# Softmax transposes of a decoder layer: from TensorE to 32x32 pieces on VectorE, blocks 2 to 7

## What is computed

```
h   = rms_norm(x, ln_mix_g) @ w_in
y_a = rms_norm(spatial_gating(h[..., :IN_A], ...), grp_norm_a)      # chunks of 128 tokens
y_b = rms_norm(short_gated_conv(h[..., IN_A:], conv_w), grp_norm_b) # width 3, causal
x   = x + concatenate([y_a, y_b], -1) @ w_out
# cross-attention, 4 heads, 256 memory tokens
q = rms_norm(x, ln_attn_g) @ w_q ; k, v = split(memn @ w_kv)
s = einsum("bshd,bmhd->bhsm", q, k) * scale
p = softmax(s, axis=-1)
x = x + einsum("bhsm,bmhd->bshd", p, v) @ w_o
# SwiGLU
g, u = split(rms_norm(x, ln_ffn_g) @ w_gate_up)
x = x + (silu(g) * u) @ w_down
return rms_norm(x, ln_final_g)
```

## Time and profile before

| what | before |
|---|---|
| median of 3 runs | 1652.73 us |
| profiled execution, own time | 1653.19 us |
| its span, slowest core (others from 1637.3) | 1651.7 us |
| TensorE busy | 1599.9 us, 97% |
| VectorE busy | 879.0 us, 53% |
| ScalarE busy | 725.9 us, 44% |
| mean granted TensorE clock, slowest core | 0.990 |
| matmuls of L1178 (transposes) | 256 |

### The profile page before, as it was taken

One profiled execution on the slowest core, in us unless ns is written; L12 is line 12 of the kernel. 1 busy time (PEld: TensorE's weight loads), 2 busy tenths in 40 slices (PEclk: granted clock), 3 DMA queues, 4 the chain that ended last, 5 costly groups with the idle time before them and its releaser, 6 DMA issues.

```text
span 1651.7 us, 22422 instructions; the slowest of 8 cores (1637.3 to 1651.7 us)
## 1 busy us (share of the span) xinstructions
PE 1599.9 (97%) x7916; PEld 758.7 (46%) x7916; DVE 879.0 (53%) x1414; ACT 725.9 (44%) x1291; POOL 76.0 (5%) x152
## 2 busy tenths in 40 slices
PE   5988999999899999999999999999999999999997
PEld 2454444444344444444444444444444444444456
DVE  4777783246455565636655565456645466433324
ACT  3644655114375246543464435554455434531221
POOL 2000000010000000000000000000000000000000
PEclk9999999999999999999999999999999999999999
DMA  9785847879997898889867994658747375334741
GB/s 213 115 167 131 205 96 130 147 129 202 214 226 124 163 222 236 169 165 176 240 183 189 168 236 176 209 119 176 234 178 232 97 183 197 128 112 155 254 168 52
DMA packets 44349, 285.64 MB, mean 173 GB/s; under 512 B 4944, under 2 KB 6992, under 8 KB 21200
## 3 DMA queue, kind: packets, MB, share of 16 engines
q0 software_dynamic: 20032, 122.95, 43.4%
q1 hardware_dynamic: 24208, 161.26, 27.5%
HBM read 365.20 MB, written 38.27 MB: 244 GB/s over the span
## 4 chain that ended last, share of the span: by engine, by line
PE 91%; DMA 7%; ACT 1%; DVE 1%; issue 1%; POOL 0%; DVEq 0%; SPq 0%; ACTq 0%; POOLq 0%
PE ps L614 64%; PE ps L1400 16%; PE ps L1127 7%; PE ps L1388 2%; DMA big<-x 2%; DMA big<-w_gate_up 2%; DMA big<-w_v 1%; DMA big<-w_qT 1%; PE ps L1178 1%; DMA big<-w_down 1%; PE ps L690 0%; DVE big L744 0%; PE ps L1069 0%; PE ps L1463 0%; DMA fold<-big 0%
## 5 line engine op out<-in xcount | busy, mean ns | idle before, releaser
L614 PE MATMUL ps<-big 128*128 128x512 bf16 (+1 forms) x5280 | 1158.0, 379 | 17.7 <-DVE big L820 5.4
L614 PEld LDWEIGHTS ps<-big 128*128 128x128 bf16 x5280 | 517.1, 98 | 626.6 <-issue 33.9
L662 ACT ACTIVATE big<-big 128x512 f32<-128x512 f32 (+1 forms) x320 | 192.0, 610 | 375.0 <-DVE big L940 256.5
L1400 PE MATMUL ps<-big 128*128 128x512 bf16 (+1 forms) x1424 | 278.8, 354 | 0.7 <-DMA big<-w_down 0.7
L1334 DVE TENSOR_TENSOR big<-ps,big 128x512 bf16<-128x512 f32 x176 | 120.4, 689 | 225.5 <-PE ps L614 176.8
L940 DVE TENSOR_TENSOR big<-ps,big 128x512 f32<-128x512 f32 x184 | 127.1, 691 | 167.9 <-PE ps L614 84.5
L672 DVE TENSOR_TENSOR big<-big 128x512 f32<-128x512 f32 (+2 forms) x272 | 178.8, 666 | 59.7 <-ACT big L662 56.5
L1400 PEld LDWEIGHTS ps<-big 128*128 128x128 bf16 x1424 | 138.9, 98 | 132.3 <-issue 1.6
L744 DVE SCALAR_TENSOR_TENSOR big<-big 128x512 bf16<-128x512 f32 (+3 forms) x256 | 172.0, 721 | 48.0 <-ACT big L702 31.8
L1328 ACT ACTIVATE big<-ps 128x512 f32<-128x512 f32 x176 | 102.8, 594 | 161.5 <-PE ps L614 158.7
L1127 PE MATMUL ps<-big 128*128 128x512 bf16 x512 | 115.2, 379 | 0.0
(11 more groups left out here) (89 smaller groups left out, 635.9 us busy)
## 6 DMA issues: line engine op xcount, KB each, us to landing
big<-gu SPq DMA_DIRECT2D x56, 1024.0 KB, 6.4
big<-w_gate_up POOLq DMA_DIRECT2D x32, 1024.0 KB, 11.4
big<-fold SPq DMA_DIRECT2D x28, 1024.0 KB, 7.1
big<-w_down POOLq DMA_DIRECT2D x36, 704.0 KB, 8.5
big<-w_cv POOLq DMA_DIRECT2D x28, 768.0 KB, 8.4
big<-dn SPq DMA_DIRECT2D x28, 704.0 KB, 5.9
big<-w_out POOLq DMA_DIRECT2D x14, 1024.0 KB, 13.8
y<-big SPq DMA_DIRECT2D x7, 2048.0 KB, 10.9
```

Of the source, the lines that this page charges most:

```text
L614: ins = e.matmul(b, lhsT=ws[k], rhs=rs[k], start=(k == 0), stop=(k == nk - 1))
L662: act((lambda e: e.activation(out=sq, in_=src, func=AF.Square)), [src], [sq], Tn)
L1400: ins = e.matmul(b, lhsT=w[:, k, :], rhs=hb[:, k, lo:hi], start=(k == 0), stop=(k == KF - 1))
```

## The change

For blocks 2 to 7 (i >= DT0 = 2) `tr` and `ev` are gone. Instead, after each second tile (NG = 2), a thread of its own puts 16 VectorE transposes (`flip`). Flip (q, jm) takes 32 partitions (32 tokens, group q) of both tiles, and of every 128-column chunk k the 32 columns of group jm: 2 x 8 blocks of 32x32, 512 elements in each of 32 partitions, in bf16. It writes the transposed blocks to partitions 32 jm and following of pTb, so that all 16 together make the full transposes of two tiles. The pair's flips may be planned only once both tiles' softmax threads are empty. The pnb slot of a tile is now fixed (`take(t)`), and is given back after the last flip. Blocks 0 and 1 keep TensorE's transposes. OFF2, the starting progress of stage 2, goes from 1.2 to 1.1.

```diff
+        def take(self, i):
+            self.free.remove(i)
+            return i
+    DT0, NG = 2, 2
...
             def mx():
-                box["r"] = r = pn_bufs.get()
+                box["r"] = r = pn_bufs.get() if i < DT0 else pn_bufs.take(t)
...
-            th.put("dve", mx, [b2], 1024, pn_bufs)
+            th.put("dve", mx, [b2], 1024, pn_bufs, gate=lambda: i < DT0 or t in pn_bufs.free)
...
-            th.put("pe", tr, lambda: [pnb[:, box["r"], :]], 0.65, banks, gate=lambda: state.get("vod", -1) >= i - 1)
-            th.put("any", ev, lambda: [banks.ap(box["t"])], 1024)
+            if i < DT0:
+                th.put("pe", tr, lambda: [pnb[:, box["r"], :]], 0.65, banks,
+                       gate=lambda: state.get("vod", -1) >= i - 1)
+                th.put("any", ev, lambda: [banks.ap(box["t"])], 1024)
+            elif t % NG == NG - 1:
+                tq = Thread(1)
+                self.tiles.append(tq)
+                for q in range(4):
+                    for jm in range(4):
+                        tq.put("dve", (lambda q=q, jm=jm: self.flip(t - NG + 1, q, jm)), [], NG * 256,
+                               gate=lambda: not any(h_.items for h_ in self.soft[t - NG + 1:t + 1]))
+
+        def flip(self, t, q, jm):
+            src = pnb[32 * q:32 * q + 32, t:t + NG, :].rearrange("p t (k j b) -> p t k j b", j=4, b=32)[:, :, :, jm, :]
+            dst = pTb[32 * jm:32 * jm + 32, t:t + NG, :].rearrange("p t (k i b) -> p t k i b", i=4, b=32)[:, :, :, q, :]
+            dve((lambda e: e.transpose(dst, src)), [pnb[:, t:t + NG, :]], [pTb[:, t:t + NG, :]], NG * 256)
+            if q == 3 and jm == 3:
+                for r in range(t, t + NG):
+                    pn_bufs.put(r)
...
-    OFF2, PRP0, PRPP = 1.2, 0.25, 33.0
+    OFF2, PRP0, PRPP = 1.1, 0.25, 33.0
```

More of the change, by code:

```diff
@@ L959, in __init__ @@
             self.tiles = []
+            self.soft = []
         def vpart(self, w_v, after):
@@ L1132, in score @@
             self.tiles.append(th)
+            self.soft.append(th)
             box = {}
             def mx():
-                box["r"] = r = pn_bufs.get()
+                box["r"] = r = pn_bufs.get() if i < DT0 else pn_bufs.take(t)
                 dve((lambda e: e.tensor_reduce(out=nmx[:, r, :], in_=b2.rearrange("p (h m) -> p h m", h=4), axis=AX.X,
```

## The result

The changed kernel takes 1678.12 us (median of 4 runs, 1676.43 to 1679.68), the kernel before 1652.74 beside it. The ratio is 1.0152, with a 95% interval of 1.0135 to 1.0170: 25 us slower, where 8 us faster was forecast, and outside the range. In some executions one die of the chip ran at a lower clock; the ratios leave these out, and of the one-flip version in experiment 1 only two executions remain.

A forecast was written before the change was run, and what follows sets the result against it. TensorE was taken as the bound: 10.8 us for removed transposes plus 1.4 for an eviction wait, less 4 for lateness, gives 8.2 us off 1653.19, so 1645.0 us; OFF2 counted as nothing; range 1637 to 1661.

The forecast's parts named there:

- What bounds the kernel: Whole kernel: TensorE is busy 1599.9 of 1651.7 us and never stops for two thirds of it.
- the removal: Blocks 2 to 7: 24 tiles' transposes leave TensorE, 10.8 us, plus an eviction wait of 1.36 us: 12.2 us.
- The price of a flip: VectorE, blocks 2 to 7: 0.70 us each, 0.8 us start to start, 154 us over the kernel.
- Rival D: VectorE's flips writing over partition groups are slow, deciding from about 0.95 us each: 1653 to 1660, or 1700; chance 0.13.
- The two row groups: VectorE in the earlier trace: three dependent additions 0.79 us apart, two untied operations 0.60 us apart.
- the 9.6 us worked out for that: A pair's 16 flips on VectorE, if a semaphore costs nothing extra: 9.6 us, and never late.
- TensorE needs 13 to 15 us of other work. It has it: Before the late value product, worked out in block 5: 24 us of gate/up matmuls and 38 us of down projection provide cover.
- I take 0.7 us a block: Blocks 2 to 7: TensorE's waits from late VectorE flips, 6 x 0.7 = 4 us in all.
- the planner's missing 0.105 us a flip: Planner prices a flip at 0.695 us: 1.7 us short over the last 16, against 2.1 us of slack.
- I take nothing: OFF2's effect on the weight wait near 430 to 460 us counted as zero, bounded at 6.5 us gain or loss.
- Rival E: At 400 to 460 us, stage 2 ahead meets full DMA engines; TensorE waits 5 to 10 us more: 1650 to 1657; chance 0.11.
- C: Each block waits 1.5 to 2.5 us at the value product or a bank, 9 to 15 us: 1650 to 1656; chance 0.14.

The follow-up runs named there:

- one-flip version: Changed kernel with OFF2 1.2 and 15 of each pair's 16 flips left out, against the kernel before: ratio 0.9917, -13.7 us.
- experiment 1: Against the kernel before: all flips with OFF2 1.2, 1.0075; OFF2 1.1 with TensorE's transposes kept, 1.0126; OFF2 1.2 with one flip of 16 kept, 0.9917.

## Why the prediction was wrong, step by step

- **What bounds the kernel, and the removal: right.** 12.2 us were priced, 13.7 measured.
- **The price of a flip: right.** 0.70 us and 0.80 from start to start were forecast from the earlier trace rows; 0.703 and 0.81 were measured. Rival D, a slow operation, is out. The unit's blocks written over other groups of partitions cost nothing extra. VectorE is busy for 1005 us and not for the 1030 forecast, because 154 us were counted with the gaps between the flips; the instructions themselves take 134.9. What the Trainium skill ("VectorE: DVE Perf Modes", The DRAIN you can't avoid) says, that a semaphore costs nothing extra, is measured there on a row of eight copies. The two row groups that the prediction set against it differ in operation as well as in the semaphore, and every flip waits for the one before by a semaphore and starts 0.1 us after its end; so no run here shows what flips would take without one, nor the 9.6 us worked out for that.
- **"TensorE needs 13 to 15 us of other work. It has it": the first step that failed.** The work was there: 19 us in block 5 passed without a wait. But the cover was counted in matmuls and not in what they read. In the changed kernel it is the down weights that come late there, by 3.9 and 3.5 us in blocks 3 and 4; with the same plan and SyncE's transfers at a quarter these waits are 0.5 and 1.0 us. At OFF2 1.2 it is the gate/up weights: such groups in a dense run use 1 MB of weights each 6.9 us (32 matmuls x 0.216), through a ring of three slots; in blocks 2 to 4, where a part is still converted from float32, a load comes 5.5 to 6.6 us late in each of these blocks (experiment 1). Half of these bytes takes 10.6 us off.
- **"I take 0.7 us a block" of lateness, 4 us: right in the waits, mis-sized in the cost.** In the changed kernel TensorE's waits for VectorE after 460 us are 4.7 us, and 5.8 with a quarter of the bytes. But the clock behind them was left out of the sum: with a quarter of the bytes it adds 4.6 us, which makes 10.4. That such a wait can bring a clock loss was said under OFF2, and not counted. At OFF2 1.2 the waits themselves are three times the forecast. The mechanism was named, with the planner's missing 0.105 us a flip, but counted for the last 16 flips alone and set against 2.1 us of slack. Where both pairs keep VectorE full, all 32 flips may add up (32 x 0.11 = 3.5 us, with the shortfall of the chain on top) against one slack of MARGIN; that sum is worked out, what the runs show is the effect of the price. Measured there without load waits: 4.6, 4.4, 2.7 and 0.4 us, 12.1 in all; with the price put right, 1.5.
- **OFF2, "I take nothing", bound of 6.5 us either way: the second step that failed, and the larger one.** It costs 20.8 us alone. The sign of being wrong that the prediction names, waits for weights before 460 us that move by more than 4 us, is there: 4.3 have become 16.6. The bound was taken from the wait that was there, as if it could only vanish or double. What should have been read is which transfers follow from stage 2 being ahead: the y store and then the x load, 2 MB each, and that from 430 to 460 no DMA capacity was left (the share is 0.99 over 400 to 460 as well). The room seen in 235 to 410 is not where the demand went.
- **Rival E** named the place and kind of this loss, at 5 to 10 us more and a chance of 0.11; at that place it is 10.8 us more of wait, with a clock loss of 2 us as before, and there is more at 638 and later. C named the lateness at 9 to 15 us in all; that is what it is at OFF2 1.2 once loads are out of the way. Neither had all of it, and no rival joined the two.
- The two edits do not add: +12.4 and +20.8 give 33.2, and together they are +25.1. On top of OFF2 1.1 the flips cost 4.3 us where the sum had them gain 8.2. With quarter bytes OFF2 1.1 helps the flips by 9 us. Why the lateness is less there was read from the traces only (down groups take part of the cover); it was not tested by itself.

## What to carry to other kernels

When a step on the bound engine's path becomes longer and other work is to fill in, price the filler by all that it consumes, its weights above all: pulling it forward is a burst of demand on the DMA queues, and here it hit in the blocks whose weights still came by converting loads. An offset between two streams that looks like a mere tuning constant moves every store and the load that follows it; list those transfers, with sizes, against the DMA share of the stretch where they will land. And when a wait for one resource is found, take that resource out altogether before saying that it is the cause: here a second, late producer stood behind the same wait, and was not to be seen in the trace.

## What the runs showed of the hardware that was not expected

- VectorE's transpose of 32 partitions x 512 bf16 elements takes 690 to 709 ns over the 192 of the changed kernel (mean 703), nearly the same as a plain operation of 512 elements (means of 686 to 691), though the output of 12 of every 16 goes to another group of partitions.
- A converting load of 1 MB that lands in 12.0 us in the median took 35 us when a 2 MB load, a 1 MB load and a 1 MB store of SyncE were on their way as well; with SyncE's transfers cut to a quarter, the DMA share of the stretch was still 0.96, the load took 20 us, and it was late by 1.7 us only. With half of its own bytes and SyncE's whole, it took 29.6 us.
- The same wait of 2.38 us near 240 us is followed by 40 matmuls in 10.48 us in some executions and cores and in 8.79 in others. A wait of that length costs 1.7 us of clock or nothing.
